# Differential attention: a batch of transposes ahead of the first map's scores on TensorE

## The reference

```python
def block(args):                       # 128 queries at a time
    qb, bi = args
    qpos = bi * BLOCK + jnp.arange(BLOCK, dtype=jnp.int32)
    bias = table[:, t5_bucket(kpos[None, :] - qpos[:, None])]
    sc = jnp.einsum('bqhmd,bkhmd->bmhqk', qb, k).astype(jnp.float32) * scale + bias[None, None]
    p = jax.nn.softmax(sc, axis=-1)    # two maps m, each over 2048 keys
    a = p[:, 0] - lam * p[:, 1]
    return jnp.einsum('bhqk,bkhd->bqhd', a.astype(v.dtype), v)
```

## Time and profile before

| what | value |
| --- | --- |
| time, median of 3 runs | 3998.1 us (3988.44 to 4002.08) |
| profiled execution | 3997.88 us, its span 3995.7 us |
| TensorE matmul, weight load busy | 95%, 66% of the span |
| VectorE, ScalarE, GpSimd busy | 55%, 44%, 57% of the span |
| differential attention | 1180 to 1660 us and 3176 to 3655 us of the span |

### The profile page before, as it was taken

The page is one execution under the profiler, slowest core; times in us unless marked ns, Lnnn a source line. Parts: engine busy times, 40 slices in busy tenths (PEclk is TensorE's granted clock), DMA queues, the critical chain, the costliest instruction groups (busy, mean ns, idle before and its releaser), DMA issues. The chain is left out here.

```text
span 3995.7 us, 52425 instructions
## 1 busy us (share of the span) xinstructions
PE 3795.6 (95%) x19002; PEld 2643.9 (66%) x19002; DVE 2180.7 (55%) x3977; ACT 1747.1 (44%) x3142; POOL 2294.9 (57%) x1381
## 2 busy tenths in 40 slices
PE   8999999999989999889989999999999899998898
PEld 8789774555546666557787897755555466665577
DVE  3003025655559999775530020255555599997755
ACT  3112103333349999761031021023333499997610
POOL 1221325877768999635512212257777689996355
PEclk9999999999999999999999999999999999999999
DMA  5434445232420222335353344432224202223353
GB/s 182 127 132 118 144 139 122 65 84 56 108 46 15 58 58 59 78 103 180 137 178 124 125 126 137 140 79 56 56 61 103 50 11 58 58 59 83 106 177 132
DMA packets 180871, 392.49 MB, mean 98 GB/s; under 512 B 18014, under 2 KB 100168, under 8 KB 168968
## 3 DMA queue, kind: packets, MB, share of 16 engines
q1 hardware_dynamic: 179752, 387.75, 34.6%
q10 hardware_dynamic: 864, 1.41, 0.2%
HBM read 255.93 MB, written 135.67 MB: 98 GB/s over the span
## 5 line engine op out<-in xcount | busy, mean ns | idle before, releaser
L1307 POOL TENSOR_TENSOR mla_sum_pool<-mla_sum_pool,mla_probs 128x1024 f32<-128x1024 f32 (+1 forms) x336 | 777.8, 2315 | 210.7 <-ACT mla_probs L1268 185.8
L1325 DVE TENSOR_REDUCE carry_row_max<-psum 128x1 f32<-128x512 f32 x688 | 474.6, 690 | 418.2 <-PE psum L1140 413.3
L1268 ACT ACTIVATE mla_probs<-psum 128x1024 f32<-128x1024 f32 x384 | 373.3, 1021 | 695.8 <-PE psum L1177 688.5
L1703 POOL TENSOR_TENSOR diff_probs<-diff_probs 128x1024 f32<-128x1024 f32 x252 | 597.1, 2369 | 100.5 <-ACT diff_probs L1647 90.0
L1635 ACT ACTIVATE diff_probs<-psum,diff_shift 128x1024 f32<-128x1024 f32 x384 | 425.7, 1115 | 11.2 <-DVE diff_shift L1730 10.0
L642 PE MATMUL psum<-in_x_hi,in_w_hi 128*128 128x512 f32 x1024 | 409.0, 399 | 2.7 <-ACT in_mla_val L749 2.7
L642 PE MATMUL psum<-in_x_hi,in_w_lo 128*128 128x512 f32 x1024 | 405.6, 396 | 0.0
L642 PE MATMUL psum<-carry_firsts,in_w_hi 128*128 128x512 f32 x1024 | 405.2, 396 | 0.0
L1190 PE MATMUL psum<-mla_probs,mla_v_op 128*64 128x512 f32 x1536 | 375.6, 610 | 0.0
L1574 PE MATMUL psum<-ident,diff_probs 128*128 128x128 f32 x2048 | 319.7, 279 | 15.3 <-DVE diff_turned L1765 8.4
L1720 DVE TENSOR_REDUCE diff_part_shift<-psum 128x1 f32<-128x1024 f32 x256 | 311.4, 1218 | 27.3 <-PE psum L1548 18.9
(11 more groups left out here) (220 smaller groups left out, 7390.4 us busy)
## 6 DMA issues: line engine op xcount, KB each, us to landing
in_w_raw<-in_w_in SPq DMA_DIRECT2D x64, 512.0 KB, 4.0
split_d<-in_out SPq DMA_DIRECT2D x64, 512.0 KB, 2.7
raw_d<-in_out SPq DMA_DIRECT2D x32, 512.0 KB, 2.7
mq_d<-in_out SPq DMA_DIRECT2D x48, 256.0 KB, 3.5
mk_d<-in_out SPq DMA_DIRECT2D x48, 256.0 KB, 4.0
carry_firsts<-split_d SPq DMA_DIRECT2D x48, 256.0 KB, 8.2
carry_weights<-split_d SPq DMA_DIRECT2D x48, 256.0 KB, 7.7
carry_weights<-split_d SPq DMA_DIRECT2D x16, 768.0 KB, 17.7
```

Of the source, the lines that this page charges most:

```text
L1268: nc.scalar.activation(probs[:, s % RING, :].rearrange("p (a n) -> p a n", n=CH), psum[:, S0 + 2 * (s % 2):S0 + 2 * (s % 2) + 2, :], ACT.E ...
L1307: nc.gpsimd.tensor_tensor(acc, start, probs[:, s % RING, mine], ALU.add).then_inc(pool_added, 1)
L1325: nc.vector.tensor_reduce(row_max[:, u % 2, qb, n:n + 1], psum[:, sweep_bank(g), :], AX.X, ALU.max).then_inc(maxed, 1)
L1703: nc.gpsimd.tensor_tensor(probs[:, n % DEEP, at], probs[:, n % DEEP, at], second, ALU.add).then_inc(mixed, 1)
```

## The change

In TensorE's turn n, `turns(n - LAG - 1, 1)`, the second batch of transposes of unit n - 3, stands ahead of `scores(n, 0, 0)` instead of between it and `scores(n, 0, 1)`. The two halves of the first map's scores then follow each other. Everything else, the other engines' orders and all waits among it, is as it was.

```diff
                 for n in range(UNITS + DRAIN + 2):
                     on = n < UNITS
+                    turns(n - LAG - 1, 1)
                     if on:
                         scores(n, 0, 0)
-                    turns(n - LAG - 1, 1)
-                    if on:
                         scores(n, 0, 1)
                     turns(n - LAG - 1, 2)
                     products(n, 0)
```

## The result

The changed kernel takes 4005.28 us (median of 12 runs, 4001.97 to 4011.52) against 3997.63 us (12 runs, 3988.44 to 4003.18) before: a ratio of 1.0024, with a 95% interval of 1.0016 to 1.0032. It is slower by 6 to 13 us. The median, 0.24%, is just under the 0.3% that the forecast called slower, and 7.65 us is about half of the 16 us that it named. The span of the profiled execution went from 3995.7 to 4005.2 us.

What follows compares the result with a forecast made beforehand. Hand-overs between four engines above 90% busy bound the kernel. Eight heads at 2.1 us made 16.7, first heads took it to 15.1, split bands added 1 to 2: +16 on 3997.88, 4014 us; 8 in 10 range 4002 to 4025.

Steps and rivals of the forecast that it cites:

- T1's wait for C0's end: TensorE: second batch of four transposes waits for ScalarE's copy of the first batch, starting 0.75 us after that copy's start.
- S1a at 1.16: TensorE: the first map's first half of scores starts 1.16 us after ScalarE's first copy starts, behind the moved transposes.
- S1b at 2.06: TensorE: the first map's second half of scores can start 2.06 us after ScalarE's first copy starts, instead of 1.75.
- The maxima at 2.26: VectorE: the maximum over the first half of scores begins no sooner than 2.26 us after ScalarE's first copy starts; before, 1.85.
- E1a at 4.88: ScalarE: the first map's first exponential starts 4.88 us after its first copy starts, 2.62 after the maxima begin.
- the paragraph on VectorE's chain: Blocks with band in the first half: late maxima make odd units take 7.61 us instead of 7.30, +0.31.
- The blocks without band: Blocks 9 to 15 of each head, with no band in the first half of scores: no loss and no gain.
- the 0.58 from S1b to T2: TensorE: the third batch of transposes starts 0.58 us after the first map's second half of scores, counted as running without a stop.
- the paragraph on TensorE's chain: Blocks with band in the first half: the later second half makes even units take 7.37 us instead of 7.06, +0.31.
- Dearer: Rival: VectorE's and TensorE's lateness add instead of hiding; odd units pay 0.3 us more, 4024 us; chance 0.14.
- Faster: Rival: earlier transposes remove ScalarE's wait before its second copy, 12 us at most, 3986 us; chance 0.05.
- Within 0.3%: Rival: VectorE's maximum follows sooner than modelled, only TensorE's chain is left, 10 us lost, 4008 us; chance 0.17.

Runs made afterwards that it cites:

- The first kernel above: Second batch of transposes moved ahead of the first half of scores only in blocks 1, 3, 5, 7, against the kernel before: 4005.77 us, ratio 1.0022.
- the third kernel: Second batch of transposes moved ahead of the first half of scores only in blocks 9 to 15, against the kernel before: 3997.34 us, ratio 0.9996.
- the last kernel above: Second batch of transposes moved behind both halves of the first map's scores, against the kernel before: 4172.91 us, ratio 1.0437.

## Why the prediction came out half right

**The direction and the mechanism held.** T1's wait for C0's end: 0.75 predicted, 0.74 measured. S1a at 1.16: 1.12. S1b at 2.06: 2.02. The maxima at 2.26: 2.22. E1a at 4.88: 4.86. The odd unit with 384 columns, 7.61 instead of 7.30: 7.59. The steps of the paragraph on VectorE's chain are right to 0.04, and right is the claim that it, not TensorE's, is what sets odd units. The first kernel above, with the odd blocks alone, had +8.3 us between first and last exponential in the trace, which the theory gave as 8 to 9 (with some luck: its steady heads grew by 0.93 and not 1.1, and its two first heads by 2.9 together).

**The blocks without band** keep their times, as forecast; the third kernel has +0.08 a head. That C1's freedom wins nothing there is seen in the changed kernel: behind unit 44's C0, C1 starts at 1.58 instead of 1.82, and E2b at 2.43 as before (1506.14 less 1503.71), when VectorE's shift is there.

**The term that was mis-sized** is the 0.58 from S1b to T2 in the paragraph on TensorE's chain, 2.06+0.58+4.04+0.69 = 7.37. I read it as TensorE's own spacing, 1425.84 to 1426.42. What I had not set beside it is ScalarE's row of the same time, of the kernel before:

```profile
1425.68 0.60 ACT L1657 ACTIVATE diff_turned<-psum 128x512 f32<-128x512 f32 x1
```

That is C1, and T2 starts 0.74 after it. That is what a batch takes after the start of a copy that it must wait for: T1 behind C0 in the changed kernel (1423.07 to 1423.81), T2 behind C1 in the last kernel above (1467.28 to 1468.02). T2 was waiting for C1, not running behind S1b. In the changed kernel C1 is far enough ahead (1.58, so 2.32), and T2 follows S1b at 2.49, 0.47 behind. With that and the measured 2.02 the chain is 2.02+0.47+4.01+0.69 = 7.19, the measured value. So 0.27 of S1b's lateness met 0.11 of slack that I had counted as work. The rest of the 0.18 by which this unit was overestimated is 0.04 in S1b's start (S1a comes 0.38 after T1, and I had 0.41) and 0.03 in the 4.04. From unit 31's C0 to unit 40's the prediction has 66.79, the changed kernel 66.20. The odd units differ by 0.01 together, block 0 by 0.16, blocks 2 and 6 by 0.18 each, block 8 by 0.09, and block 4 by 0.03 the other way. Eight heads of 0.59 are 4.7 us of the 16; the kernel with the even blocks alone (+3.4 us in the trace, 7.6 by the prediction's terms) shows that it is these units. The split bands of blocks 3 and 4, for which I added 1 to 2 us, are within 0.04 of what I counted for 384 columns (7.65 and 7.40 against 7.61 and 7.37), 0.6 us in all.

**What stays open** is the rest, between the 11.25 us that the stages grew in the traces and the 7.65 us between the medians. The traces differ by 1.7 us the other way outside the stages, and the changed kernel's profiled execution, 4007.40 us, lies 2.1 us above its median. Neither can be told from chance with one execution of each, and the interval of the ratio, 6 to 13 us, holds both figures. The 0.8 us that I took off for each layer's first head did not show as such either: the first heads grew by 1.8 and 1.3 us, with a length that varies from trace to trace. In the kernel with the blocks without band they are 1.4 and 0.5 us shorter, though the steady heads are not.

**Two small slips** changed nothing. The 0.54 of a half without band does not follow from 0.90 less 0.34, which is 0.56; the rows have 0.54 from the scores to the band in the changed kernel (1424.19 to 1424.73). And S1a of unit 33 ran 0.19 after C0 before the change, not some 0.3: its band starts at 1417.52, 0.54 behind it.

**The rivals.** Dearer fell: the two chains hide behind each other, since C3, in unit 33's turn, starts 5.58 after C0 before and 5.59 after it in the changed kernel. Faster fell for the change as it stands, though not the idea behind it: T1 early without holding S1a back wins 0.5 us a head. The Trainium skill (Perfetto Trace Analysis, Optimization Strategy) says to make what the engine in question waits for start sooner. The trace with S1a divided agrees, with those 0.5 us; the one of the change does not, with +1.5. Within 0.3% came out in the time, and not by its mechanism, which was that VectorE's chain does not bind; it does. Its 4008 us is nearer to the 4005.28 than my 4014, and the lower end of my range, 4002, lay inside this rival: that the range held is in part luck.

## What to carry to other kernels

Before an instruction is moved ahead of another on an engine that works in the order of issue, as TensorE does here with S1a behind the waiting T1, ask what it waits for and what used to run during that wait. An early place for a waiting instruction is free only if what follows it has the wait's length to spare on every chain that it feeds, here 0.63 for a half of scores (S1b's 1.75 less S1a's 1.12), which 0.54 meets and 0.90 does not. If it hasn't, split the work: the part that fills the wait goes in front and the rest behind, which here turned +1.5 us a head into -0.5.

When a chain is summed from starts in a trace, test each spacing against all that the later instruction waits for, not only its neighbour. A spacing that fits a copy's start plus a known constant to 0.01 is most likely a wait, and a wait does not shift with the neighbour.

## What the runs showed that was not expected

Steady units repeat to about 0.03 us, from head to head, from layer to layer and from kernel to kernel (blocks 9 to 15 take the same time in all six traces of kernels with the band and T1 ahead of S1b), while whole executions scatter by 10 to 15 us. A head's length in one trace shows the 0.5 us that the divided S1a wins; in the times that is 0.1%, and 11 runs against 30 hardly showed it. The length of a whole stage is less sure, since the first heads vary by over 1 us.

Without the band's matmuls the stage shortens by 4.7 us a head (111.38 against 116.11) and its bound moves: GpSimd's mixing then holds back the transposes, a wait of 15.8 us a head in the changed kernel without band.
